# Expert weight units of 2 MB: one transfer each in place of two of 1 MB

## The reference

```
def swiglu(h, w_up, w_down):
    gate, up = jnp.split(h @ w_up, 2, axis=-1)
    return (jax.nn.silu(gate) * up) @ w_down

def moe_swiglu(h, w_router, b_router, w_up, w_down):
...
    for e in range(N_EXPERTS):
        out = out + combine[:, e:e + 1].astype(t.dtype) * swiglu(t, w_up[e], w_down[e])
```

## Time and profile before

| | us |
|---|---|
| three runs | 1778.63, 1783.91, 1783.85 |
| median | 1783.85 |
| the profiled execution, its own time | 1778.17 |
| its span in the trace | 1776.3 |
| TensorE busy | 1610.2 (91%) |
| VectorE busy | 1277.5 (72%) |
| ScalarE busy | 1016.3 (57%) |

### The profile page before, as it was taken

How to read it: one execution, slowest core, us unless ns; L and a number is a source line. 1 busy time by engine, 2 the same in 40 slices (tenths; PEclk the granted TensorE clock), 3 DMA queues, 4 the chain that set the end, 5 groups by cost and what they waited for, 6 DMA issues and landing times.

```text
span 1776.3 us, 19829 instructions
## 1 busy us (share of the span) xinstructions
PE 1610.2 (91%) x7776; PEld 1291.6 (73%) x7776; DVE 1277.5 (72%) x1145; ACT 1016.3 (57%) x880; POOL 108.5 (6%) x88
## 2 busy tenths in 40 slices
PE   3888996999969999749999999999999999999991
PEld 0774764878857777538888888888888888888881
DVE  1275536655465665748888889889888898888885
ACT  1332224444435444337777777777777777777773
POOL 0431310010001000210000000000000000000000
PEclk9998998999989999869999999999999999999996
DMA  9347885954445444449999999999999999999992
GB/s 331 119 161 288 309 312 186 308 189 170 150 154 186 162 142 155 154 168 375 362 381 391 368 385 383 373 386 377 375 389 366 383 383 372 385 375 376 386 370 90
DMA packets 235713, 518.47 MB, mean 292 GB/s; under 512 B 9000, under 2 KB 41024, under 8 KB 235520
## 3 DMA queue, kind: packets, MB, share of 16 engines
q1 hardware_dynamic: 229472, 494.62, 76.6%
q10 hardware_dynamic: 3136, 12.32, 1.9%
q0 software_dynamic: 3008, 10.20, 1.9%
HBM read 509.77 MB, written 13.63 MB: 295 GB/s over the span
## 4 chain that ended last, share of the span: by engine, by line
PE 80%; DVE 9%; DMA 5%; ACT 3%; issue 3%; SPq 0%; POOL 0%; ACTq 0%; DVEq 0%; POOLq 0%
PE bank L750 23%; PE bank L752 23%; PE bank L751 23%; DMA ring<-in_moe_w_up 3%; PE bank L729 2%; DVE w_lo L1609 2%; PE bank L913 2%; DMA ring<-in_cond_w 2%; ACT w_hi L1490 1%; PE bank L1166 1%; PE bank L745 1%; DVE small L1644 1%; DVE hs L1638 1%; PE bank L762 0%; PE bank L1155 0%
## 5 line engine op out<-in xcount | busy, mean ns | idle before, releaser
L1609 DVE TENSOR_TENSOR w_lo<-ring,w_hi 128x2048 fp32r<-128x2048 f32 x338 | 767.3, 2291 | 120.6 <-ACT w_hi L1490 119.9
L1490 ACT ACTIVATE w_hi<-ring 128x2048 fp32r<-128x2048 f32 x336 | 643.2, 1917 | 199.4 <-PE bank L752 144.2
L750 PE MATMUL bank<-w_lo,heT_hi 128*128 128x512 f32 x896 | 354.9, 396 | 4.3 <-DVE w_lo L1609 2.6
L752 PE MATMUL bank<-w_hi,heT_hi 128*128 128x512 f32 x896 | 350.5, 391 | 0.0
L751 PE MATMUL bank<-w_hi,heT_lo 128*128 128x512 f32 x896 | 349.7, 390 | 0.0
L1598 DVE TENSOR_TENSOR w_part<-ring,w_part 128x1024 fp32r<-128x1024 f32 x148 | 182.8, 1242 | 224.3 <-ACT w_part L1267 223.7
L1267 ACT ACTIVATE w_part<-ring 128x1024 fp32r<-128x1024 f32 (+1 forms) x162 | 169.1, 1049 | 255.8 <-PE bank L752 249.5
L750 PEld LDWEIGHTS bank<-w_lo,heT_hi 128*128 128x128 f32 x896 | 168.8, 188 | 41.8 <-issue 6.1
L752 PEld LDWEIGHTS bank<-w_hi,heT_hi 128*128 128x128 f32 x896 | 168.6, 188 | 36.0
L751 PEld LDWEIGHTS bank<-w_hi,heT_lo 128*128 128x128 f32 x896 | 168.9, 189 | 33.6
L750 PE MATMUL bank<-w_part,hT_hi 128*128 128x512 f32 (+1 forms) x448 | 179.7, 401 | 14.4 <-DVE w_part L1598 14.4
(11 more groups left out here) (326 smaller groups left out, 1538.2 us busy)
## 6 DMA issues: line engine op xcount, KB each, us to landing
ring<-in_moe_w_up SPq DMA_DIRECT2D x226, 1024.0 KB, 8.4
ring<-in_moe_w_down SPq DMA_DIRECT2D x112, 1024.0 KB, 7.1
ring<-in_cond_w SPq DMA_DIRECT2D x24, 2048.0 KB, 9.5
ring<-in_ffn_w_up SPq DMA_DIRECT2D x22, 1024.0 KB, 7.9
ring<-in_od_w_in SPq DMA_DIRECT2D x8, 2048.0 KB, 7.9
ring<-in_ev_w_in SPq DMA_DIRECT2D x5, 2048.0 KB, 12.6
ring<-in_ffn_w_down SPq DMA_DIRECT2D x5, 2048.0 KB, 7.6
ring<-in_od_w_in SPq DMA_DIRECT2D x8, 1024.0 KB, 8.0
```

The lines of the kernel that those rows point to most:

```text
L750: mm(bank, lhs[0], rhs[1], start=start, stop=False)
L752: return mm(bank, lhs[0], rhs[0], start=False, stop=stop)
L1490: f(w_hi[:, (n + 2 * late) % 3], w[:, half * PIECE:(half + 1) * PIECE], ACT.Copy) \
L1609: tt(w_lo[:, buf], at, w_hi[:, buf].bitcast(F32), ALU.subtract).then_inc(S["w_lo"], 1)
```

## The change

Each unit is fetched with one transfer of 2 MB over both halves, and the semaphore's steps per unit go from 32 to 16. The bytes, the slots, the order of the units and the length of each contiguous piece (512 floats, 2 KB, in `w_up`; 1024 floats, 4 KB, in `w_down`) stay.

```diff
         def slot_landed(eng, it, a):
 
             slot, n = a % RING, a // RING
-            eng.wait_ge(weights_in[slot], it * (32 * SLOT_USES) + (landed[slot] + 32 * n + 32))
+            eng.wait_ge(weights_in[slot], it * (16 * SLOT_USES) + (landed[slot] + 16 * n + 16))
             return ring[:, slot * UNIT:(slot + 1) * UNIT]
...
                 if u < N_UP:
                     w = moe_w_up[0, e].rearrange("(k p) n -> p k n", p=P)
                     c0 = 512 * (u // 2) + FFE * (u % 2)
-                    for half in range(2):
-                        sp.dma_start(to[:, half * PIECE:(half + 1) * PIECE].rearrange("p (k n) -> p k n", n=512),
-                                     w[:, 4 * half:4 * half + 4, c0:c0 + 512]).then_inc(weights_in[slot], 16)
+                    sp.dma_start(to.rearrange("p (k n) -> p k n", n=512), w[:, :, c0:c0 + 512]).then_inc(weights_in[slot], 16)
                 else:
-                    for half in range(2):
-                        r = 512 * (u - N_UP) + 256 * half
-                        sp.dma_start(to[:, half * PIECE:(half + 1) * PIECE].rearrange("p (k n) -> p k n", n=D),
-                                     moe_w_down[0, e, r:r + 256].rearrange("(k p) n -> p k n", p=P)) \
-                            .then_inc(weights_in[slot], 16)
+                    r = 512 * (u - N_UP)
+                    sp.dma_start(to.rearrange("p (k n) -> p k n", n=D),
+                                 moe_w_down[0, e, r:r + 512].rearrange("(k p) n -> p k n", p=P)).then_inc(weights_in[slot], 16)
```

## The result

The changed kernel takes 1787.75 us (median of 20 runs, 1783.95 to 1794.55); the kernel before takes 1783.10 us beside it (20 runs, 1777.65 to 1787.24). The ratio is 1.0032, with a 95% interval of 1.0021 to 1.0043: 4.65 us slower. The forecast was no change, with a chance of 0.11 on slower; the median lies inside the stated range, the direction was missed.

The account below looks back on a forecast made before the run. Matmuls on TensorE were taken to bound the expert stage, with DMA nearly full. The terms (second half, completion, wait, landing) were each 0, summing to 0, ends -2.0 and +2.8: forecast 1783 us, range 1776 to 1790.

Parts of the forecast that it names:

- TensorE bounds, DMA is nearly full: Expert stage: matmuls set the time, TensorE busy 886.98 of 889.00 us, while all 16 DMA engines are busy, share 1.02.
- The margin I worked out: Expert stage, per item: DMA needs 114.7 of 119.0 us, leaving 4.3 us, 0.2 us per unit, or 4%.
- One issue fewer: SyncE's queue: 169 units lose their second issue of 0.51 us, off the path and with no landing gained, 0 us.
- one completion fewer: DMA engines: dropping a completion per unit shortens nothing, as units land 5.4 us apart in one piece or two, 0 us.
- Rival B: DMA engines: each transfer has a cost after all, so ScalarE's 49.5 us of waits shrink, TensorE gains 2.0; 1781.8 us, chance 0.12.
- the time to land: Short queue early in an item: a single `w_down` transfer lands in 7.6 against 7.4 us; seven units pay 1.4 us, absorbed.
- The bound of +2.8 us: Landing price at most 0.26 us, 1.8 us over seven `w_down` units; 0.4 us reaches TensorE in each of seven items.
- a slack of 1.4 us: Early in an item ScalarE starts on a unit 1.4 us after its landing, released by TensorE and not DMA.
- Rival A: Eighth unit of each item: whole-unit transfers hold DMA engines longer and DMA becomes the bound; 12.6 us slower, 1796 us, chance 0.11.
- 0.08 us per unit: Extra DMA time per unit, 1.6% of 5.4, from which 63 such extras reach 5.3 us and decide for slower.
- the sum's own upper end: Top of the range before widening: highest of three earlier runs, 1783.9, plus 2.8 us, giving 1786.7 us.
- The gain of at most 2.0 us: Expert stage: TensorE can gain no more than its idle time, 889.00 - 886.98 = 2.0 us, the sum's lower end.

## Why the prediction was wrong, point by point

- **TensorE bounds, DMA is nearly full.** Right. The margin I worked out, 4% of the DMA's time, was right as a rate and misleading as a reserve: the kernel with earlier issues moves the same bytes with 8.8 us of waiting. The reserve was not in the rate but in how late a slot's next fetch is issued.
- **One issue fewer, one completion fewer: 0.** Right for `w_up` (0.9988) and, with rows 3.5 MB apart, for all units (1.0000). Rival B was wrong: ScalarE's waits grew.
- **The step that failed** is the one on the time to land: I priced a single `w_down` transfer at 0.2 us, 7.6 against 7.4 us, and called it absorbed. It was mis-sized. The changed kernel's `w_down` units are complete 9.7 us after issue in the median and the pairs of before after 8.7, so the price was some 1.0 us, what the queue ahead adds included. It was not absorbed either: these units brought 22.1 us of ScalarE's waiting where there was 1.9, and TensorE's wait for `w_lo` went from 1.8 to 10.5 us. The two rows were not alike. The single transfer was issued at 462.9 us, 2.4 us after the transfer ahead of it had landed; the pair that I called lone was issued at 992.65, while the unit ahead was in flight until 994.97, and it was one of the quickest. No row of before showed a single transfer of this shape behind another. The row that I used for the back-to-back case has the shape of `w_up`, and for that it held.
- **The bound of +2.8 us** rested on a slack of 1.4 us at the start of an item. It allowed for a shift of 1.8 us there. In the item shown the slack was consumed and ScalarE waits 1.63 us more, a shift of 3.0, and the loss is +4.65 us.
- **Rival A** named the place, the eighth unit of an item, and for `w_down` the mechanism, extra time per unit that adds up and reaches TensorE. Its sum was wrong: it counts the extra for every unit, and `w_up` units have none, so its 12.6 us were 8 too many against the 4.65 measured. It decides, I wrote, from 0.08 us per unit; that threshold should have had more weight than 0.11, because the only row with the pieces of `w_down` lay above it.
- **The range** of 1776 to 1790 us took in 1787.75 by its width and not by the mechanism: the sum's own upper end gave 1786.7, and the rest had been added towards rival A.
- **The gain of at most 2.0 us** also failed, as the early issue gained 7.4 us (1781.01 - 1773.64). Part of it is in the traces. The stage of the kernel with early issue, to be held against the 956.10 us of before:

```profile
783.20:1735.20 952.00, 951.17 (x4320) 786.51 (x4320) 835.46 (x464) 714.05 (x480) 0.00 (x0) 1.00 1.01 373
```

It is 4.1 us shorter, 2.0 in idle time and 2.1 in busy time for the same 4320 matmuls at the same granted clock. So the busy time of TensorE held lateness too, and idle time was no bound. For the rest, I read an execution 5 us under its kernel's median. If the other executions wait more than it did, that explains the gain; there is only one trace of the kernel before, so this is argued, not shown.

The Trainium skill, DMA: Bandwidth & Descriptors, section on latency and other measured facts, was cited for rows at power-of-two distances, and for an inferred aliasing of streams in step. The runs agree with its direction: 512 KB costs, 3.5 MB (seven times that) does not. Its table gives nearly full rate at 512 KiB, but for a distance between partitions, in copies from HBM to HBM. Here it is the distance between one partition's rows, and it was enough to lose with four rows in one transfer (1.0034 and 1.0045), not with two. That the page's cause is at work here, no run shows.

Counted from the packet records of the traces between 850 and 1700 us, the 4 KB packets usually take 0.159 us, and those that take over 0.259 rose from 983 to 1233 with the change. But with rows 3.5 MB apart, where nothing is lost, there are 1199, so their number doesn't explain the loss. What makes the transfers with rows 512 KB apart end late stays open.

## What to carry to other kernels

A larger transfer can cost even where the issues it saves are free: look at how many rows of one partition it walks in turn, and how far apart they lie. Price it from transfers of the same shape that follow on each other, not from a lone one. And where a ring of buffers feeds a full engine, releasing and refetching half a buffer at a time was worth more here (0.39%) than any size of transfer.

## What the runs showed that was not expected

Four transfers of 512 KB in place of two of 1 MB cost 0.38%, though SyncE issues them in 0.4 to 0.5 us each and a unit takes 5.4. The DMA share read 1.02 in kernels in which ScalarE waited 8.8 us for landings and 105 us.
